# A hybrid decoder layer on one core: cache copies issued later, sample values two iterations later, squares added on VectorE and the last stage's products moved into the expert blocks

## What is computed

```python
h = rmsnorm(x, g_mix)
z = h @ w_in                       # 1024 x 8704: RG-LRU x and gate, q, k, v, two merge gates
y_r = rglru(conv(z_x)) * gelu(z_g); b_lru = y_r @ w_br_lru
q, k = rope(rmsnorm(q)), rope(rmsnorm(k))
att = attend(q, k, v)              # prompt: dilated windows; sample: keys and values from the caches
b_att = att @ w_br_att
x = x + (sigmoid(g_lru) * b_lru + sigmoid(g_att) * b_att) @ w_out
x = x + moe(rmsnorm(x, g_ffn))     # router, top 4 of 32 experts, clamped SwiGLU, 12.6 MB of weights each
x = x + sigmoid(rmsnorm(x, g_ple) @ w_ple_gate) * (p @ w_ple)
```

## Time and profile before

| | |
|---|---|
| median of 3 runs | 1442.58 us (1441.81 to 1442.85) |
| the profiled execution | 1436.98 us, span of its trace 1435.2 us |
| TensorE matmuls busy | 1351.3 us (94% of the span) |
| VectorE, ScalarE, GpSimd busy | 375.8, 223.9, 17.2 us |
| moved by DMA | 530.49 MB, mean 370 GB/s |
| SyncE's queue (q1), ScalarE's queue (q10) | 470.67 MB, 54.43 MB |

### The profile page before, as it was taken

One profiled execution on the slowest core, in us unless ns is written; L12 is line 12 of the kernel. 1 busy time (PEld: TensorE's weight loads), 2 busy tenths in 40 slices (PEclk: granted clock), 3 DMA queues, 4 the chain that ended last, 5 costly groups with the idle time before them and its releaser, 6 DMA issues.

```text
span 1435.2 us, 15736 instructions
## 1 busy us (share of the span) xinstructions
PE 1351.3 (94%) x6663; PEld 694.0 (48%) x6663; DVE 375.8 (26%) x523; ACT 223.9 (16%) x395; POOL 17.2 (1%) x33
## 2 busy tenths in 40 slices
PE   6999999769998999999998999999999999999988
PEld 5787878658875333333333333333333333333337
DVE  3069715111232221221222212222121221221224
ACT  1222145124003011011010110101101011010011
POOL 0000111000000000000000000000000000000000
PEclk9999999889999999999999999999999999999999
DMA  9779999995825899999999999999999999999960
GB/s 379 291 252 397 328 379 349 305 393 194 348 77 191 342 429 427 428 426 428 428 429 428 428 429 428 429 428 428 429 428 427 430 427 428 429 427 427 426 259 31
DMA packets 50129, 530.49 MB, mean 370 GB/s; under 512 B 6029, under 2 KB 6173, under 8 KB 21221
## 3 DMA queue, kind: packets, MB, share of 16 engines
q1 hardware_dynamic: 34944, 470.67, 79.1%
q10 hardware_dynamic: 13717, 54.43, 10.7%
q0 software_dynamic: 1424, 4.76, 1.0%
HBM read 525.08 MB, written 58.38 MB: 407 GB/s over the span
## 4 chain that ended last, share of the span: by engine, by line
PE 70%; DMA 22%; DVE 3%; ACT 2%; ACTq 1%; issue 1%; SPq 0%; POOL 0%; DVEq 0%
PE PS L831 32%; DMA Zb<-in_b_gu 20%; PE PS L565 12%; PE PS L877 5%; PE PS L748 3%; PE PS L846 3%; PE PS L856 3%; PE PS L992 2%; PE PS L771 2%; PE PS L837 2%; DMA ring<-in_vt 1%; DVE ring L1279 1%; ACTq L396 1%; PE PS L578 1%; PE PS L643 1%
## 5 line engine op out<-in xcount | busy, mean ns | idle before, releaser
L831 PE MATMUL PS<-ring,Zb 128*64 128x512 f32 x2304 | 518.7, 603 | 0.8 <-ACT Zb L1191 0.8
L831 PEld LDWEIGHTS PS<-ring,Zb 128*64 128x64 f32 x2304 | 163.0, 139 | 317.6 <-issue 317.4
L565 PE MATMUL PS<-HL,ring 128*128 128x264 f32 x1024 | 233.5, 388 | 0.0
L565 PEld LDWEIGHTS PS<-HL,ring 128*128 128x128 f32 x1024 | 194.1, 191 | 32.9 <-issue 0.4
L1516 DVE COPY Zb<-PS 64x512 f32<-64x512 f32 x32 | 21.9, 683 | 363.8 <-PE PS L831 363.8
L831 PE MATMUL PS<-Zb 128*64 128x512 f32 x384 | 91.6, 621 | 0.4 <-issue 0.4
L1195 ACT ACTIVATE Zb<-Zb 128x512 f32<-128x512 f32 x32 | 20.2, 630 | 450.6 <-DVE Zb L1494 450.6
L831 PE MATMUL PS<-HL,Zb 128*64 128x512 f32 x384 | 86.9, 594 | 0.0
L1484 DVE TENSOR_TENSOR xc<-xc,PS 128x528 f32<-128x528 f32 x68 | 47.6, 701 | 101.4 <-PE PS L877 92.5
L1187 ACT ACTIVATE Zb<-PS 128x512 f32<-128x512 f32 x32 | 19.1, 597 | 352.5 <-PE PS L860 352.5
L877 PE MATMUL PS<-Zb 128*128 128x264 f32 x240 | 69.5, 412 | 0.0
(11 more groups left out here) (232 smaller groups left out, 915.5 us busy)
## 6 DMA issues: line engine op xcount, KB each, us to landing
ring<-in_wexp SPq DMA_DIRECT2D x144, 2048.0 KB, 27.5
Zb<-in_wexp SPq DMA_DIRECT2D x24, 2048.0 KB, 26.7
HL<-in_wexp SPq DMA_DIRECT2D x24, 2048.0 KB, 28.1
ring<-in_win SPq DMA_DIRECT2D x17, 2048.0 KB, 12.5
out_kvs<-in_cache ACTq DMA_DIRECT2D x8, 4032.0 KB, 39.8
out_kvs<-in_cache ACTq DMA_DIRECT2D x8, 1984.0 KB, 20.7
ring<-in_kt SPq DMA_DIRECT2D x2, 2048.0 KB, 14.8
ring<-in_vt SPq DMA_DIRECT2D x2, 2048.0 KB, 16.1
```

Of the source, the lines that this page charges most:

```text
L565: last = mm(PS[:, z_bank(n), 0:T], w[:, k, t * P:(t + 1) * P], hT[:, k, :], start=(k == 0), stop=(k == KT - 1))
L831: last = mm(PS[CAP * h:CAP * (h + 1), bank, :], src[:, k, f:f + CAP], w[:, k, h * CH:(h + 1) * CH], start=(not seeded and slot % 2 == 0 an ...
```

## The change

It has five parts.

1. **Copies.** `both(6)` moves from before `rows_out(1)` to the end of iteration 2, `both(7)` from iteration 1 to 6. Group 2's stream 4 moves from iteration 0 to 4; streams 5, 6, 7 and the three `shift_rest` move behind the last sigmoid after the iterations (before: iterations 1, 2, 3, and 4).
2. **Sample values** at iterations 1, 3 and 5 in place of 1, 2, 3, their sum at 7. SyncE issues piece 15 ahead of `vt1`, piece 16 ahead of `vt2`, and the second half of `w_br_lru` ahead of the first.
3. **Squares.** VectorE adds the eight tiles of squares (halving steps at the start; one addition per tile behind `w_out`), and TensorE multiplies one tile by ones in place of eight.
4. **`p @ w_ple`** moves behind `spread` in blocks 25, 27 and 29 (3, 3 and 2 tiles) with two banks, ScalarE's evictions with it. For it two more pairs of blocks on TensorE, three on ScalarE, are written out and no longer looped; its operands are loaded after the merge.
5. **Places.** Bias rows lie where the masks were, `yb` where the attention's output was, `plT` has a place of its own.

```diff
+PLE = ((0, 3), (3, 6), (6, 8))
@@ sync
             piece(14)
+            piece(15)
             sp.wait_ge(S.spv_mm, 1)
             sp.dma_start(stream, a["vt1"]).then_inc(S.v1_in, 16)
-            piece(15)
+            piece(16)
             sp.wait_ge(S.spv_mm, 2)
             sp.dma_start(stream[:, 0:2048], a["vt2"]).then_inc(S.v2_in, 16)
-            piece(16)
+            sp.wait_ge(S.z_done, 4 * 15)
+            half(a["w_br_lru"], 4, wbl[1], S.wbl_in)
             sp.wait_ge(S.spv_mm, 3)
             half(a["w_br_lru"], 0, wbl[0], S.wbl_in)
-            sp.wait_ge(S.z_done, 4 * 15)
-            half(a["w_br_lru"], 4, wbl[1], S.wbl_in)
@@ tensor
-            def sum_sq(src, nth):
+            def sum_sq(bank, src, nth):
                 pe.wait_ge(S.sq_ok, nth)
-                for k in range(KT):
-                    last = mm(PS[:, 4, 0:T], ones, src[:, k, :], start=(k == 0), stop=(k == KT - 1))
-                last.then_inc(S.ss_sum, 1)
+                mm(PS[:, bank, 0:T], ones, src[:, 0, :], start=True, stop=True).then_inc(S.ss_sum, 1)
...
-                if 1 <= it <= 3:
-                    stream_values(it - 1)
-                if it == 5:
+                if it in (1, 3, 5):
+                    stream_values(it // 2)
+                if it == 7:
...
                     mm(PS[0:E, 1, 0:T], wr[:, m - 2, :], Z[:, m - 2, :], start=(m == 2), stop=(m == KT + 1))
-                    last = mm(PS[:, 0, 0:T], ones, lt[:, m - 2, :], start=(m == 2), stop=(m == KT + 1))
-            last.then_inc(S.ss_sum, 1)
+            sum_sq(0, lt, 2)
...
-            pe.wait_ge(S.wpl_in, 32)
-            pe.wait_ge(S.ht_ev, 2)
-            ple_tiles(0, 4)
...
-            ple_tiles(4, KT)
...
                 if prev:
                     spread(j, 3)
+                if ple is not None:
+                    pe.wait_ge(S.added, 4 * j + 4)
+                    ple_tiles(*ple)
                 if following:
                     rows(n + 1, j + o, 1 - o)
...
-            with pe.Fori(1, E // 4 - 1) as q:
+            with pe.Fori(1, E // 4 - 2) as q:
                 for odd in range(2):
                     pair(q, odd)
-            pair(E // 4 - 1, 0)
+            pair(E // 4 - 2, 0, ple=PLE[0])
+            pair(E // 4 - 2, 1, ple=PLE[1])
+            pair(E // 4 - 1, 0, ple=PLE[2])
@@ scalar
-            both(6)
             rows_out(1)
...
-                if it == 1:
-                    both(7)
-                if it < 4:
-                    shift(act, 2, it + 4)
+                if it in (2, 6):
+                    both(it // 4 + 6)
                 if it == 4:
-                    for g in range(NG):
-                        shift_rest(act, g)
+                    shift(act, 2, 4)
             act.wait_ge(S.z_evac, NZ)
             A(Z[:, ZGA:ZGA + KT, :], Z[:, ZGA:ZGA + KT, :], ACT.Sigmoid).then_inc(S.sig_z, 1)
+            for b in (5, 6, 7):
+                shift(act, 2, b)
+            for g in range(NG):
+                shift_rest(act, g)
@@ vector
+            def add_tiles(sq):
+
+                for n in (4, 2):
+                    link(TT(sq[:, 0:n, :], sq[:, 0:n, :], sq[:, n:2 * n, :], ALU.add))
+                TT(sq[:, 0, :], sq[:, 0, :], sq[:, 1, :], ALU.add).then_inc(S.sq_ok, 1)
```

More of the change, by code:

```diff
@@ L333, in build @@
         cmax, most = zb([1, 1]), zb([1, 1], I32)
[L334 to L335 removed]
+        wpl, pT = zb([P, 2, D]), zb([P, 2, T])
+        plT = zb([P, KT, T])
+        assert pos[0] <= NZ * T, pos[0]
         sgp = Z[:, 0:KT, :]
@@ L494, in _ @@
             sp.dma_start(slot(3), weights(0, 3)).then_inc(S.w3, 16)
+            sp.wait_ge(S.merged, KT)
+            sp.dma_start(wpl, a["w_ple"].rearrange("(k p) n -> p k n", p=P)).then_inc(S.wpl_in, 16)
+            sp.dma_start(pT, a["pT"]).then_inc(S.wpl_in, 16)
             sp.wait_ge(S.wo_mm, KT)
@@ L797, in ple_tiles @@
             def ple_tiles(m0, m1):
+                if m0 == 0:
+                    pe.wait_ge(S.wpl_in, 32)
                 for m in range(m0, m1):
-                    if m >= 4:
-                        pe.wait_ge(S.pl_ev, m - 3)
+                    if m >= 2:
+                        pe.wait_ge(S.pl_ev, m - 1)
                     for k in range(2):
-                        last = mm(PS[:, 2 + m % 4, 0:T], wpl[:, k, m * P:(m + 1) * P], pT[:, k, :],
+                        last = mm(PS[:, 2 + m % 2, 0:T], wpl[:, k, m * P:(m + 1) * P], pT[:, k, :],
                                   start=(k == 0), stop=(k == 1))
                     last.then_inc(S.pl_mm, 1)
-            pe.wait_ge(S.wpl_in, 32)
-            pe.wait_ge(S.ht_ev, 2)
-            ple_tiles(0, 4)
             pe.wait_ge(S.oh_ready, 1)
@@ L934, in block_ @@
                 half_product(4, hmT, r, 5, seeded=False).then_inc(S.d1_mm, 1)
+                if ple is not None:
+                    pe.wait_ge(S.pl_ev, ple[1])
             def spread_all(j):
@@ L982, in _ @@
                 if m == 2:
-                    pe.wait_ge(S.sq_ok, 2)
-                    mm(PS[:, 4, 0:T], ones, lt[:, 0, :], start=True, stop=True).then_inc(S.ss_sum, 1)
+                    sum_sq(4, lt, 3)
                 if m == 3:
@@ L1174, in _ @@
                   scale=sm[0:nt, 40 + b:41 + b]).then_inc(S.ht_ev, 1)
-            for m in range(KT):
-                act.wait_ge(S.pl_mm, m + 1)
-                A(plT[:, m, :], PS[:, 2 + m % 4, 0:T], ACT.Copy).then_inc(S.pl_ev, 1)
             act.wait_ge(S.rt_exp, 1)
@@ L1191, in rows_T_copy, with block_ @@
                 A(xgT, tiles(6), ACT.Copy).then_inc(S.xT_ok, 1)
-            def block_(n, j, o, following=True):
+            def block_(n, j, o, following=True, ple=None):
                 act.wait_ge(S.gmin, n + 1)
                 A(ss_, sg, ACT.Sigmoid, scale=ALPHA).then_inc(S.sig, 1)
+                if ple is not None:
+                    for m in range(*ple):
+                        act.wait_ge(S.pl_mm, m + 1)
+                        A(plT[:, m, :], PS[:, 2 + m % 2, 0:T], ACT.Copy).then_inc(S.pl_ev, 1)
                 if following:
@@ L1209, in _ @@
             A(gateT, PS[0:E, 7, 0:T], ACT.Copy).then_inc(S.gt_ok, 1)
-            with act.Fori(0, E // 2 - 1) as j:
+            with act.Fori(0, E // 2 - 4) as j:
                 block_(2 * j, j, 0)
                 block_(2 * j + 1, j, 1)
+            for i in range(3):
+                j = E // 2 - 4 + i
+                block_(2 * j, j, 0)
+                block_(2 * j + 1, j, 1, ple=PLE[i])
             block_(E - 2, E // 2 - 1, 0)
@@ L1545, in _ @@
             link(TT(lt[:, :, :], xc[:, :, :], xc[:, :, :], ALU.mult))
-            for n in (4, 2):
-                link(TT(lt[:, 0:n, :], lt[:, 0:n, :], lt[:, n:2 * n, :], ALU.add))
-            TT(lt[:, 0, :], lt[:, 0, :], lt[:, 1, :], ALU.add).then_inc(S.sq_ok, 1)
+            add_tiles(lt)
             v.wait_ge(S.rms_ok, 3)
```

27 lines of the change are left out of this document (15 added, 12 removed).

## The result

The changed kernel's median is 1407.59 us (1406.47 to 1410.48) against 1442.59 us for the kernel before, run beside it: the ratio is 0.9761, with a 95% interval of [0.9744, 0.9778]. By the ratio that is 34.5 us saved, between 32.0 and 36.9; the two medians differ by 35.0. The profiled execution took 1410.48 us with a span of 1408.7, so the two traces differ by 26.5 us only: the one before happened to lie 5.6 us under its median, the one after 2.9 us above its own.

A forecast was written before the change was run, and what follows sets the result against it. From 495 us DMA of the experts' weights sets the pace, so TensorE time saved before 458 us counts one for one. Savings of 3.2 + 13.3 + 1.9 + 3.5 + 4.8 = 26.7, less 1.0, give 1416.9 us; range 1406 to 1428.

The forecast's parts named there:

- the first rival: Attention: the sample values arrive in time, saving 6.5 and 1.7 us more; 33.9 saved, 1408.7 us; chance 0.28.
- the 5.8: Router: `rows(0)` can start near 447.1 and not 452.91, 5.8 us earlier, before 1.0 is taken off for slower TensorE.
- The start, 3.2: First norm: one product with ones replaces eight, saving 3.2 us; VectorE's additions hidden under TensorE's first tile by 3.3 us.
- The full queue, 13.3: Attention: left-over copies moved behind it free ScalarE, saving TensorE's 12.1 us wait and 1.2 of slow restart.
- the sample values, 1.9: Attention: later use cuts the 8.4 us wait for `in_vt` only to 6.5, saving 1.9; the slow restart stays.
- it is not the copies that are slow in it: Attention's 110 GB/s stretch of 12 us follows `out_hp`'s small stores; copies run at normal rates elsewhere, so the stretch returns.
- Behind w_out, 3.5: After `w_out`: fewer products with ones save 3.3 us between tiles and 0.2 after the last, together 3.5.
- The router, 4.8: Router: moving `p @ w_ple` out starts `rows(0)` 5.8 us earlier, less 1.0 for slower TensorE after pauses: 4.8 saved.
- The experts, lost 1.0: Blocks 25, 27, 29: the moved tiles take 7.6 us, mostly covered by bias-row waits; 1.0 lost.
- The bytes fit: Before the expert stream: 16.4 MB of copies take 40 us at 410 GB/s, within 48.4 us of idle DMA; 0 lost.
- The bytes did not collide: Rival: copies reach into the expert stage (5 us) and `ple_tiles` cost 7.6; 14.1 saved, 1428.5 us; chance 0.19.
- the full queue did not come back: Rival, attention: `both(7)` at iteration 6 meets a full queue, ScalarE stands again; 13.3 lost, 1430.2 us; chance 0.03.

The follow-up runs named there:

- start_eight: Changed kernel with the first norm's eight products with ones back on TensorE and VectorE's three additions there gone; median 1410.67 us, ratio 0.9793.
- copies_only: The kernel before with part 1 (the cache copies' new places) alone, sample values still at iterations 1, 2, 3; median 1417.66 us, ratio 0.9847.
- values_first: Changed kernel with `vt1` issued ahead of piece 15 again, still multiplied at iteration 3; median 1401.28 us, ratio 0.9710.
- warm: Changed kernel with filler products, results unused, in TensorE's two router pauses (eight, then two); median 1401.44 us, ratio 0.9726.
- ple_router: Changed kernel with the eight `p @ w_ple` tiles back in the router and out of blocks 25, 27, 29; median 1412.82 us, ratio 0.9796.
- copies_back: Changed kernel with part 1 undone, cache copies at their old places, the four other parts kept; median 1428.35 us, ratio 0.9917.
- h_late: Changed kernel with the tiny stores of the last recurrent state issued after the last iteration, not at 251 us; median 1401.58 us, ratio 0.9718.

## Why the prediction was right, and where not

The forecast of 1416.9 us was 9.3 above the median, inside its range; faster was right. That the range held it was in part luck. The median lies below the forecast's own 1411 to 1422, and only the lower end that was set for the first rival covers it. That rival with all of the 5.8 saves 34.9 by its own terms and gives 1407.7, not 1406; the median of 1407.59 is at that edge. By its steps:

- **The start, 3.2.** Measured 3.9 by start_eight, near 3 by the traces. Right, the cover too; the changed kernel, VectorE's last addition and TensorE's product:

```profile
12.94 0.43 DVE L1261 TENSOR_TENSOR HL<-HL 128x264 f32<-128x264 f32 x1
```

```profile
17.27 0.61 PE L553 MATMUL PS<-HL,cst 128*128 128x264 f32 x2
```

- **The full queue, 13.3, and the sample values, 1.9.** This is where the sum failed. Together 15.2, while the copies alone measured 22.6 and the attention stretch shrank by 19.9 in the first pair of traces and 21.2 in the second. Two things were wrong. The 12.1 us of the earlier trace rows were one execution's draw (another read 15.0), and I took them as the size. And I split what has one cause: by copies_only, thinning the copies frees ScalarE and lets `vt1` through in time. The step "it is not the copies that are slow in it" was true, since the stores make the stretch, and yet no ground for leaving them out: `vt1` and the copies share what passes before and in the stretch, and the copies took 2.00 of 4.56 MB there. With the copies gone, `vt1` at its old place was not waited for at all. The 0.7 MB that the forecast let pass in the stretch has no row of its own either; the earlier trace rows give 110 GB/s for 12 us, 1.3 MB.
- **The later place of the values** is then no gain but a small loss: behind piece 15, `vt1` can go only when piece 15's place is free. The forecast named this queue and put the issue at 252.7 and the wait at 6.5; the traces have 256.22 and 3.5, and 253.83 and 3.2. In the second TensorE asked at 271.96, as worked out (271.5), and the values were there at 275.2, not 278.0. Mechanism right, size off by 3. The kernels without the wait are 3.4 to 7.4 us faster by their saved times (38.4 to 40.9 against 33.5 and 35.0). In the traces the attention stretch is 89.8 and 89.5 us with it and 84.6 without: 5.2 and 4.9. Of the 5.2, the wait is 3.5 and the slow restart behind it 1.7 (L613 2.61 against 1.93, L657 1.65 against 0.94, the next group of L566 7.55 against 7.29). The idea of the later use was sound all the same: with the load left ahead of piece 15 (values_first) the stretch is 84.6, with the old use and the old place (copies_only) 88.5. Only the load's move behind piece 15 lost that gain.
- **Behind w_out, 3.5.** From the first `dense` product to the transposes it is 77.9 us in every trace with this part and 80.8 or 80.9 in every one without: 2.9. Near enough; not tried alone.
- **The router, 4.8.** The mechanism was right: `rows(0)` starts 12.6 and 11.9 us after the transposes start, against 16.4 and 18.1 before, so 3.8 to 6.2 earlier with 5.8 forecast. That the first trace has it at 426.2 as forecast is luck: there the start had saved nothing by 178 us and the attention more than its term, and the second trace has it at 422.8. The clock's share was set too low. From the transposes to the end of the first expert's product, both traces of before take 26.9 us, the changed kernel 24.4 and 23.8, and warm 21.1. So 5.8 are there to be had, as worked out from the earlier trace rows, and the clock takes 2.7 to 3.3 of them, more than the 2.0 I had as its upper bound. The term of 4.8 was 2.5 to 3.2.
- **The experts, lost 1.0.** Nothing was lost. From that product's end to the end of the span it is 970.7 and 968.3 us, against 971.8 and 971.7 before; the bias waits fell from 24.6 to 19.8 and took the tiles in. The gain of 1 to 3.5 us belongs to part 4, since ple_router, with the tiles back, reads 971.8; how it comes about isn't shown. It made up for the router: part 4 as a whole was forecast at 3.8 and measured 4.1 to 5.6. Two errors cancelled there.
- **The bytes fit.** Share 0.90 in 331 to 430, experts at 425 GB/s. ScalarE was held until 399.3, forecast 398.

The parts by the experiments: 22.6 for the copies, 3.9 for the start, 4.1 to 5.6 for part 4, 2.9 behind w_out from the traces: 33.5 to 35.0, against 33.5 and 35.0 measured. That leaves about nothing for the values' new place; the agreement is closer than the noise of such parts, 1 to 2 us each.

The first rival, sample values in time, came nearest in time (1408.7), but the values were late. Its reason, that much of `vt1`'s 20.8 us was the copies', is what copies_only showed; the load's new place behind piece 15 kept it from coming true. The bytes did not collide and the full queue did not come back in the attention.

## What to carry to other kernels

Where two waits of TensorE stand close together and one queue feeds both, cost the queue's load as one term and try it alone first; a wait of one execution is a draw, and a second trace of the same kernel costs little. Before moving an operand's use later, look at what its load is queued behind: the load moved as well, and the later use paid, 3.9 us, only where the load kept its place ahead of them. And work taken out of a pause on TensorE leaves a pause: what follows it may run at half clock, and ten unused products in it gave back some 3 us.

## What the hardware showed that I had not expected

- Two stores of 36 KB together from strided columns held the core's DMA at 37 to 55 GB/s for 6 us in the changed kernel (share up to 1.10), and 43 to 107 for 9 us in copies_back, where the copies run beside them; after a copy into adjacent columns on VectorE they landed in 1.7 us, not 7.3, with no slow stretch at all, although the profile counts the same number of packets under 512 B (6029) for both.
- An engine that issues DMAs can stand for a long time on a full queue: 57 to 71 us for three small copies behind large ones. It cost nothing only because the engine's next work was due later, 13.2 us later here and 3.6 us later in h_late.
- The clock fell to its lower level after a pause of 3.6 us on TensorE and cost some 3 us behind it. When it falls varies from trace to trace: in the second trace after, the first three rank products still ran at 0.41 and 0.39 us and the next at 0.61. In the second trace of before the first expert's product ran at full clock (3.65 us), in the first at 5.35, with the router's tiles 1.7 us faster in turn, so that the stretch was 26.9 in both. Such a balance is chance: in copies_only both are slow (5.49 and 5.35), and the same stretch takes 28.6.
